# Expert gathers issued in turns, one U row and one V row, instead of four U rows and then four V rows

## What is computed

```python
def block(args):
    hb, ib, gb = args
    act = jax.nn.gelu(jnp.einsum('td,tkd->tk', hb, p['peer_u'][ib]))
    return jnp.einsum('tk,tkd->td', act * gb, p['peer_v'][ib])
```

## Time and profile before

| what | value |
|---|---|
| time of three executions | 3452.19, 3455.93, 3461.99 us |
| median | 3455.93 us |
| span of the profiled execution | 3455.3 us |
| PE busy | 3200.0 us, 93% |
| DVE busy | 1851.0 us, 54% |
| POOL busy | 918.8 us, 27% |
| ACT busy | 525.4 us, 15% |
| moved by DMA | 989.40 MB, of which 536.90 MB by the gathers' queue |

### The profile page before, as it was taken

The page is one execution under the profiler, slowest core; times in us unless marked ns, Lnnn a source line. Parts: engine busy times, 40 slices in busy tenths (PEclk is TensorE's granted clock), DMA queues, the critical chain, the costliest instruction groups (busy, mean ns, idle before and its releaser), DMA issues. The chain is left out here.

```text
span 3455.3 us, 30801 instructions
## 1 busy us (share of the span) xinstructions
PE 3200.0 (93%) x10108; PEld 1775.5 (51%) x10108; DVE 1851.0 (54%) x3355; ACT 525.4 (15%) x1056; POOL 918.8 (27%) x618
## 2 busy tenths in 40 slices
PE   6999999999999999999999999998987887878876
PEld 2467667575857576777644444443433333333332
DVE  6544444444444344666756434656566566565655
ACT  2312212121212121211000001111111111111110
POOL 0011112020202111100000002555555555555553
PEclk8999999999999999999999999999998898898988
DMA  9764554545463645545554597999999999999997
GB/s 359 288 227 179 188 185 175 200 169 209 149 231 132 231 163 205 205 170 192 200 180 170 171 342 296 398 427 423 427 421 423 423 426 424 426 427 427 426 427 311
DMA packets 152449, 989.40 MB, mean 286 GB/s; under 512 B 17771, under 2 KB 30764, under 8 KB 38572
## 3 DMA queue, kind: packets, MB, share of 16 engines
q0 software_dynamic: 73728, 536.90, 37.0%
q1 hardware_dynamic: 67104, 424.88, 33.9%
q10 hardware_dynamic: 11536, 26.55, 2.0%
HBM read 969.13 MB, written 19.14 MB: 286 GB/s over the span
## 5 line engine op out<-in xcount | busy, mean ns | idle before, releaser
L2535 PE MATMUL ps<-gates,diagonal 128*128 128x512 f32 x2048 | 992.2, 647 | 198.6 <-ACT diagonal L2163 198.6
L1075 PE MATMUL ps<-mT,ring 128*128 128x256 f32 (+1 forms) x4096 | 1168.9, 446 | 1.1 <-PEq L216 1.1
L1075 PEld LDWEIGHTS ps<-mT,ring 128*128 128x128 f32 x4096 | 775.0, 190 | 387.9 <-issue 318.2
L2352 DVE CUSTOM_DVE_ANT_0 u_rows<-u_rows,yhy 128x2048 f32<-128x2048 f32 x256 | 585.9, 2292 | 470.4 <-DMA u_rows<-in_peer_u_dram,expert_index 458.3
L2535 PEld LDWEIGHTS ps<-gates,diagonal 128*128 128x128 f32 x2048 | 420.5, 208 | 768.7 <-issue 637.9
L2096 POOL DMA_INDIRECT gates<-in_peer_v_dram,expert_index x256 | 418.9, 1636 | 502.8 <-PE ps L2535 417.3
L2096 POOL DMA_INDIRECT u_rows<-in_peer_u_dram,expert_index x256 | 273.6, 1069 | 135.8 <-issue 134.6
L707 POOL TENSOR_TENSOR dd<-mask_f,dt_g 128x1024 f32<-128x1024 f32 x16 | 30.3, 1896 | 933.0 <-DVE dt_g L977 932.4
L867 DVE SCALAR_TENSOR_TENSOR conv<-ps,tap_g,conv 128x510 f32<-128x510 f32 (+1 forms) x48 | 33.8, 704 | 338.7 <-ACT conv L728 338.7
L2157 ACT ACTIVATE gelu<-dot 128x4 f32<-128x4 f32 x64 | 13.1, 205 | 1059.2 <-DVE dot L2352 1059.2
L881 DVE SCALAR_TENSOR_TENSOR ada_sums<-ada_tiles,csil,ada_sums 128x1024 f32<-128x1024 f32 x120 | 153.9, 1283 | 4.0
(11 more groups left out here) (372 smaller groups left out, 2878.2 us busy)
## 6 DMA issues: line engine op xcount, KB each, us to landing
ring<-in_w_stream_dram SPq DMA_DIRECT2D x160, 1024.0 KB, 5.0
ada_tiles<-in_w_ada_dram SPq DMA_DIRECT2D x64, 1024.0 KB, 6.8
ring<-in_w_mix_dram SPq DMA_DIRECT2D x48, 1024.0 KB, 4.9
ring<-in_w_mod_dram SPq DMA_DIRECT2D x32, 1024.0 KB, 10.7
ring<-in_w_out_dram SPq DMA_DIRECT2D x32, 1024.0 KB, 5.4
rows<-cum_rows_scratch SPq DMA_DIRECT2D x16, 1536.0 KB, 13.1
ring<-in_w_q_dram SPq DMA_DIRECT2D x11, 1024.0 KB, 7.2
hf_scratch<-hf ACTq DMA_DIRECT2D x8, 768.0 KB, 6.4
```

What stands on the lines that cost most here:

```text
L1075: mm = nc.tensor.matmul(ps[:, k % 4, 0:n], m.ring[:, slot, kt * P:(kt + 1) * P], m.mT[:, kt, 0:n], start=(kt == 0), stop=(kt == KT - 1))
L2352: nc.vector.tensor_tensor_reduce(out=u_slot[n], in0=u_slot[n], in1=h2[:, t, :], scale=1.0, scalar=0.0, op0=ALU.mult, op1=ALU.add, accum_ou ...
L2535: return nc.tensor.matmul(ps[:, 4 * t + b, :], dia[:, (h % 2) * S + n, :], v_slot[n][:, b * CH:(b + 1) * CH], start=first and n == 0, stop ...
```

## The change

On POOL, the loop over the four slots n becomes the outer loop and the pair U, V the inner one. Before, a batch's gathers were issued as U0 U1 U2 U3 V0 V1 V2 V3; now as U0 V0 U1 V1 U2 V2 U3 V3. Each gather keeps its own wait, and all other streams stay as they were.

```diff
                     for h in range(NB):
                         pool.wait_ge(idx_v, NB * u + (h + 1))
-                        for slots, table, into, free in ((u_slot, d.peer_u, u_in, u_free), (v_slot, d.peer_v, v_in, v_free)):
-                            for n in range(S):
+                        for n in range(S):
+                            for slots, table, into, free in ((u_slot, d.peer_u, u_in, u_free), (v_slot, d.peer_v, v_in, v_free)):
                                 pool.wait_ge(free, TOPK * u + (S * h + n + 1))
 
                                 if slots is u_slot and n == 3:
```

## The result

| | before | changed |
|---|---|---|
| median | 3456.14 us | 4046.63 us (4046.39 to 4047.09) |
| span of the profiled execution | 3455.3 us | 4045.3 us |
| ratio | | 1.171, 95% interval 1.169 to 1.172 |

A forecast was written before the change was run, and what follows sets the result against it. The prediction took DMA transfers as the bound; the change closes a loop from U3 to the next U3: 3.57 + 7.42 + 3.8 + 14.7 = 29.5 us a batch, and 2195 + 8 + 63 x 29.5 = 4061.5 us, range 3930 to 4190.

The forecast's parts named there:

- What bounds the kernel: In the gather stage the DMA transfers are the bound: DMA share 1.01 at 424 GB/s, 20.0 us a batch.
- Step 1: From U3's landing through dot product, gelu, coefficients to PE's first matmul of the batch: 3.57 us.
- Step 2: From PE's first matmul to POOL's issue of V0: 7.42 us after long idle, low end 6.21.
- Step 3: Transfers in line behind U3: only its batch's V3 and the next U0, 4.9 us, then the engines are dry.
- Step 4: Restarting the dry DMA engines after V0's issue costs between 3.05 and 4.5 us, taken as 3.8.
- V0's own landing: Sign for the restart of the DMA engines: V0 should land near 6.2 us after its issue.
- Step 5: From V0 to U3 on the gathers' queue: six rows of transfer, 14.7 us, with issues keeping ahead.
- The sum: A batch takes 29.5 us instead of 20.0; with 63 batches, the rest and 8 us in batch 0, 4061.5 us.
- The clock rival: TensorE keeps the high clock at a batch's start: 26.6 us a batch, 3879 us; chance 6%.
- The slower rival: TensorE's lower clock covers row 1 too, V1 issued 6.9 us after V0: 31.5 a batch, 4188 us; chance 11%.
- What the trace would show: In the gather stage: DMA share about 0.67, about 285 GB/s, V0 waits some 8 us or more, PE clock under 0.91.
- DVE holding up the issue: On POOL, a dot product delays V0's issue by a microsecond at most, in one batch of four: 15 us in all.

The follow-up runs named there:

- Opening the loop: Coefficients made from the gates alone, ahead of the dot products: 3474.5 us in the changed kernel's order, 3454.8 us in the order of the kernel before.

## Why the prediction was right

- **What bounds the kernel** held. Opening the loop gave 19.62 us a batch in either order.
- **Step 1**, U3 to the first matmul: 3.57 forecast, 3610.60 - 3607.03 = 3.57 measured. The mean of the 63 batches, read from the timelines of DVE, PE and POOL like those below, is 3.39: most batches of tile 0 take 3.22.
- **Step 2**, first matmul to V0: 7.42 forecast. It is 3618.00 - 3610.60 = 7.40 in one batch and 3646.52 - 3640.32 = 6.20 in the next; PE's batches take 16.7 to 17.0 and 15.4 to 15.9 us, mostly by turns, after idle times of 12 to 15 us in tile 1. The mean of the 63 is 6.74: the term was 0.68 us too long. The shorter value had stood in the rows before, as the low end 6.21.
- **Step 3**, what covers: two rows. Two rows from 3607.03 end at 3611.9, and the window from 3612 to 3618 with a DMA share of 0.00 shows the engines dry from there to V0.
- **Step 4**, restart: 3.8 forecast. From V0 at 3618.00 to U3 at 3636.76 are 18.76 us, less six rows of 2.45: 4.06; in the next batch, by its period of 28.88, 4.4. The mean of the 63 is 4.40, so this term was 0.60 us too short: the 4.5 lost over five gathers in the earlier trace rows was the better guide than the 3.05 of a single one. V0's own landing, the sign named for this step, is not in the trace; the dot product of U1, the row behind it, starts 8.92 us after V0's issue, two rows and 4.0. The page DMA: Bandwidth & Descriptors of the Trainium skill (section Anatomy of one DMA) would make it 2.0 by its fixed cost; the row on dry engines, 5.2 us for one gather, 2.75 more than its transfer, speaks against that for these gathers.
- **Step 5**, six rows at 2.45: as forecast, inside the sum above.
- **The sum.** A batch took 3.39 + 6.74 + 4.40 + 14.7 = 29.22 us in the mean against 29.5: 63 x 0.28 = 18 us less. That it came so near is in part luck, as steps 1 and 2 were 0.86 us too long together and step 4 was 0.60 too short; with step 4 alone right the forecast would have been 4099, with steps 1 and 2 alone right 4007, both still in the range. Batch 0 was 10.9 us later instead of 8 (its gelu starts at 2174.55 against 2163.63), and the end after the last gelu was 1.5 us shorter: 4061.5 - 18 + 3 - 1.5 = 4045, the measured span.
- **The clock rival** named a true mechanism that didn't come to pass by itself: the run that kept PE busy came down to 27.35 us a batch, near its 26.6. The slower rival did not come to pass: V1 is issued 3621.44 - 3618.00 = 3.44 us after V0, not 6.9.
- **What the trace would show** did, with small misses: DMA share 0.72 where 0.67 was forecast, 290 GB/s for 285, waits of 15 to 16 us at V0 for "8 or more", granted clock 0.78. Query weights are only a small part of the first miss: from 3255 to 4015, behind them, the share is 0.71 at 286 GB/s. More of it is share without rate while the engines restart: from 3648 to 3649 it is 0.87 at 156 GB/s.
- **DVE holding up the issue** was rightly small here: V0 behind a batch with rank_pairs took 1.19 us at 3618.00 instead of 0.94, and at most 2.48, half a microsecond over the bound of the prediction.

## What to carry to other kernels

In a queue that issues in program order, a transfer that waits for a slot blocks all behind it, also those whose slots are free; ask for each how long the work is that frees its slot, and put ahead of it enough transfers that don't depend on that work to last as long. Here 9.8 us of wait behind eight rows cost nothing, and about 11 us behind two rows cost 590 us. If two streams are to be mixed, mix the late one from the batch before, and then the order costs next to nothing (9 us here).

## What the runs showed of the hardware

After idle times of the same length, 12.4 to 13.2 us, PE's batches start mostly by turns with a slow stretch worth 1.4 to 1.9 us and one worth 2.6 to 3.0 (batches of 15.4 to 15.9 and 16.6 to 17.0 us, against 14.0); in the earlier trace rows only the longer one had been seen after a long idle. In the kernel before, the same two lengths come after idles of only 4.20 us (15.69) and 3.93 us (16.70). An idle of 3.11 us was followed by a slow start, and in the run with 14 more matmuls one of 2.56 us; the idles of 0.5 to 1.8 us there were not (granted clock 0.99). In the kernel before, 2.19 us were followed by 14.00 us once and by 15.66 once, so the length of the idle alone does not tell. And a stream of 1.05 MB gathers that has run dry pays 4.4 us in the mean until it is back in step (4.0 to 4.6 in the middle half of 63 batches), more than the 3.05 us by which a single row's landing exceeds its transfer.
